# A gate taken third, state sums ahead of the convolution, and one product for both scan directions in the first layer

## The reference, cut to what matters

```python
xs, bm, cm = split(silu(conv5(x @ w_in[...]) + bias))  # 32 heads of 64, 8 groups of 4 heads, state 128
z = x @ w_in[...]                                      # the gates
xc = xs * dt                                           # dt differs between the two directions
cs = cumsum(dt * a)                                    # within chunks of 128 tokens
cb   = einsum('bclgn,bcsgn->bclsg', cc, bc)
lmat = exp(where(lower, cs[l] - cs[s], -inf))
y = einsum('bclsg,bclsgr,bcsgrp->bclgrp', cb, lmat, xc) \
  + einsum('bclgn,bcgrpn,bclgr->bclgrp', cc, h_in, exp(cs))
h = h * exp(cs_end) + einsum('...', bc, decay_to_end, xc)   # the state handed from chunk to chunk
ssd = rmsnorm((y_forward + y_backward + d * xs) * silu(z)) @ w_ssd_o
```

## Time and profile before

| | us |
|---|---|
| median of 3 runs | 2936.31 (2933.43 to 2937.91) |
| the profiled execution's own time | 2936.1 |
| its span, first to last instruction | 2934.3 |
| PE busy | 2833.2, 97% of the span |
| DVE busy | 871.6, 30% |
| ACT busy | 722.1, 25% |
| POOL busy | 325.7, 11% |

### The profile page before, as it was taken

How to read it: one execution, slowest core, us unless ns; L and a number is a source line. 1 busy time by engine, 2 the same in 40 slices (tenths; PEclk the granted TensorE clock), 3 DMA queues, 4 the chain that set the end, 5 groups by cost and what they waited for, 6 DMA issues and landing times.

```text
span 2934.3 us, 30410 instructions
## 1 busy us (share of the span) xinstructions
PE 2833.2 (97%) x12082; PEld 1794.3 (61%) x12082; DVE 871.6 (30%) x1656; ACT 722.1 (25%) x1696; POOL 325.7 (11%) x326
## 2 busy tenths in 40 slices
PE   7989998999999998999999999999999999999999
PEld 6778884555555565444444444444665677788888
DVE  1330005555455333200121000005667632211101
ACT  1330012555455333100010000003445422101100
POOL 3000001233233121000000000000122222000000
PEclk8999999999999999999999999999999999999999
DMA  9236775433332121222262442425444322357652
GB/s 235 81 100 186 196 199 135 115 101 98 87 101 67 51 58 44 58 79 79 72 179 74 129 131 75 129 75 132 115 103 108 91 67 73 96 153 222 173 151 86
DMA packets 530156, 330.37 MB, mean 113 GB/s; under 512 B 27504, under 2 KB 496864, under 8 KB 530016
## 3 DMA queue, kind: packets, MB, share of 16 engines
q1 hardware_dynamic: 519184, 296.36, 36.7%
q0 software_dynamic: 10528, 31.46, 4.4%
q10 hardware_dynamic: 304, 0.61, 0.1%
HBM read 327.05 MB, written 1.34 MB: 112 GB/s over the span
## 4 chain that ended last, share of the span: by engine, by line
PE 82%; ACT 8%; DVE 5%; issue 2%; PEld 1%; DMA 1%; DVEq 1%; POOL 0%; PEldq 0%; POOLq 0%; ACTq 0%; SPq 0%
PE ps L972 61%; PE ps L1345 4%; PE ps L1336 4%; PE ps L1327 3%; ACT TMP L797 2%; PE ps L1311 2%; DVE TMP L1870 2%; PE ps L1432 2%; PE ps L998 1%; PE ps L1455 1%; ACT TMP L803 1%; ACT BIG L809 1%; PE ps L982 1%; PEld ps L972 1%; DMA BIG<-bias_lines 1%
## 5 line engine op out<-in xcount | busy, mean ns | idle before, releaser
L972 PE MATMUL ps<-xnT,W 128*128 128x512 f32 (+2 forms) x4064 | 1327.3, 486 | 15.2 <-DVE TMP L1652 6.7
L972 PEld LDWEIGHTS ps<-xnT,W 128*128 128x128 f32 (+1 forms) x4064 | 771.7, 191 | 530.5 <-issue 448.1
L972 PE MATMUL ps<-BIG,W 128*128 128x256 f32 (+1 forms) x2528 | 772.4, 467 | 5.3 <-DVEq L401 2.7
L972 PEld LDWEIGHTS ps<-BIG,W 128*128 128x128 f32 x2528 | 480.4, 191 | 290.8 <-issue 245.9
L1870 DVE SCALAR_TENSOR_TENSOR TMP<-ps,prmT,TMP 128x510 f32<-128x510 f32 (+3 forms) x256 | 181.9, 714 | 106.1 <-ACT TMP L776 91.4
L612 ACT ACTIVATE xnT<-hT 128x512 f32<-128x512 f32 (+1 forms) x48 | 25.2, 525 | 563.4 <-DVE hT L1801 464.4
L1801 DVE SCALAR_TENSOR_TENSOR hT<-ps,modc,hT 128x256 f32<-128x256 f32 x48 | 21.8, 481 | 373.6 <-PE ps L972 373.6
L564 POOL TENSOR_TENSOR BIG<-BIG,TMP 128x512 f32<-128x512 f32 x80 | 106.6, 1348 | 191.5 <-ACT BIG L809 191.5
L2072 DVE TENSOR_TENSOR BIG<-TMP 128x512 f32<-128x512 f32 (+1 forms) x64 | 35.8, 559 | 301.8 <-ACT TMP L942 301.8
L1345 PE MATMUL ps<-W,xnT 128*128 128x128 f32 x1024 | 122.8, 276 | 0.0
L797 ACT ACTIVATE TMP<-BIG,TMP 128x128 f32<-128x128 f32 x384 | 117.4, 392 | 12.4 <-PE ps L1311 12.4
(11 more groups left out here) (274 smaller groups left out, 2144.3 us busy)
## 6 DMA issues: line engine op xcount, KB each, us to landing
W<-in_w_in SPq DMA_DIRECT2D x192, 512.0 KB, 4.0
W<-in_w_mlp SPq DMA_DIRECT2D x128, 512.0 KB, 4.1
W<-in_ada_w SPq DMA_DIRECT2D x96, 512.0 KB, 3.8
BIG<-cs_rows POOLq DMA_DIRECT2D x96, 256.0 KB, 4.8
W<-in_w_ssd_o SPq DMA_DIRECT2D x32, 512.0 KB, 3.7
W<-in_w_gate SPq DMA_DIRECT2D x22, 512.0 KB, 5.8
W<-in_w_up SPq DMA_DIRECT2D x22, 512.0 KB, 6.0
W<-in_w_down SPq DMA_DIRECT2D x16, 512.0 KB, 3.8
```

What stands on the lines that cost most here:

```text
L972: last = mm(dst, w[:, c, 0:m], rhs(k), start=k == 0, stop=k == total - 1)
```

## The change

Six edits. The first four are in layer 0 alone.

1. For groups 1 to 7, z0 is made third: x0, x1, z0, B, C, z1. Both gates then go to bank PS[0], where B's product goes too (`early_z`, `front_order`). The weights are ordered to match. z0 waits for the convolution of x0, B for the first gate, z1 for the convolution of B.
2. On ACT the first gate and the activation of x0 move ahead of `decays(g, 2)`.
3. Both directions go into one product: `xc` is copied, and `masked` takes layer 1's form (eight instructions of 128 columns and an addition instead of two of 512 columns).
4. On DVE `masked(g, 3)` moves ahead of `conv(g+1, 2)`.
5. In both layers `carried(g, 0)` and `decayed(g, 2)` move ahead of `conv(g+1, 0)` on DVE.
6. In both layers the last group's pieces of the attention head are spread differently on PE: between its `outputs` (two steps between the last two, and in layer 0 two more between the first two). Two buffers of the attention (`va0`, `qkt`) get a place of their own in SBUF in place of one that the gates use.

The two new functions:

```diff
+def early_z(l, g):
+
+    return l == 0 and g > 0
+
+
+def front_order(l, g):
+    return (0, 1, 4, 2, 3, 5) if early_z(l, g) else range(6)
```

ACT, in the loop over groups:

```diff
                         center(g + 1, 1)
+                        if l == 0:
+                            gated(g + 1, 0)
+                            activated(g + 1, 0)
...
-                        for t in range(4):
+                        for t in range(0 if l else 1, 4):
                             activated(g + 1, t)
-                        for t in range(2):
+                        for t in range(0 if l else 1, 2):
                             gated(g + 1, t)
```

PE, `front` and `outputs`:

```diff
                 def front(g, t):
-                    if t >= 2:
+                    b = 0 if early_z(l, g) and t == 5 else t % 2
+                    if early_z(l, g) and t == 4:
+                        R("conv", 4 * g + 1)
+                    elif early_z(l, g) and t == 5:
+                        R("conv", 4 * g + 3)
+                    elif early_z(l, g) and t == 2:
+                        R("gated", 2 * g + 1)
+                    elif t >= 2:
                         R("conv", 4 * g + t - 1)
                     elif g:
-                        R("gated", 2 * (g - 1) + t + 1)
+                        R("gated", 2 * (g - 1) + (2 if early_z(l, g - 1) else t + 1))
...
-                        for d in range(1 if l else 2):
-                            terms.append([(xc[:, d, ch, h * HD:(h + 1) * HD], mt[:, (2 * (n_ch * g + i) + d) % 4, h, :])
-                                          for h in (2 * pair, 2 * pair + 1)])
+                        terms.append([(xc[:, ch, h * HD:(h + 1) * HD], mt[:, (2 * (n_ch * g + i)) % 4, h, :])
+                                      for h in (2 * pair, 2 * pair + 1)])
```

PE, in the loop over groups:

```diff
                     if more:
                         front(g + 1, 1)
+                        if l == 0:
+                            front(g + 1, 4)
...
                     if l == 0:
                         outputs(g, 0)
+                        if not more:
+                            next(head0)
+                            next(head0)
                         outputs(g, 1)
                     states(g, 2)
                     if more:
                         front(g + 1, 2)
                         front(g + 1, 3)
                     else:
-                        for _ in range(4):
+                        for _ in range(2 if l == 0 else 4):
                             next(head0)
                     outputs(g, 0 if l else 2)
+                    if not more:
+                        next(head0)
+                        next(head0)
                     outputs(g, 1 if l else 3)
                     if more:
-                        front(g + 1, 4)
+                        if l:
+                            front(g + 1, 4)
                         front(g + 1, 5)
```

DVE, `masked` and the loop over groups:

```diff
-                        if l == 0:
-                            V.tensor_tensor(mt[:, c % 4, :, :], mt[:, c % 4, :, :],
-                                            cbm[:, d, order[i], :].unsqueeze(1).to_broadcast([P, 4, P]), ALU.mult)\
-                                .then_inc(ssd[l, "mready"], 1)
-                            continue
...
                     masked(g, 0)
+                    carried(g, 0)
+                    decayed(g, 2)
                     if more:
                         conv(g + 1, 0)
-                    carried(g, 0)
-                    decayed(g, 2)
                     dve.drain()
...
                     if l == 0:
                         masked(g, 2)
+                        masked(g, 3)
                     if more:
                         conv(g + 1, 2)
-                    if l == 0:
-                        masked(g, 3)
-                    if more:
                         conv(g + 1, 3)
```

More of the change, by code:

```diff
@@ L195, in weight_tiles @@
         for g in range(NG):
[L196 to L198 removed]
+            at = (SSD_X + g * 256, SSD_X + P + g * 256, SSD_B + g * P, SSD_C + g * P, SSD_Z + g * 256, SSD_Z + P + g * 256)
+            for t in front_order(l, g):
+                col(("ssd", l, g, FRONT[t]), wi, at[t])
         for h in range(8):
@@ L786, in gated @@
                         R("y1", 2 * (g - 2) + 2)
-                    A(zs[:, g % 2, t, 0:n_tok], PS[t][:, 0:n_tok], ACT.Silu).then_inc(ssd[l, "gated"], 1)
+                    b = 0 if early_z(l, g) else t
+                    A(zs[:, g % 2, t, 0:n_tok], PS[b][:, 0:n_tok], ACT.Silu).then_inc(ssd[l, "gated"], 1)
                 def decays(g, i):
@@ L1958, in _ @@
                         R("ychunk", n_ch * g)
[L1959 to L1968 removed]
+                    for b in range(n_ch // 2):
+                        last = V.tensor_copy(flat(xc[:, 2 * b:2 * b + 2, :]), PS[4 + b][:, :])
                     last.then_inc(ssd[l, "xc"], 1)
```

26 lines of the change are left out of this document (5 added, 21 removed).

## The result

The changed kernel takes 2903.24 us, median of 4 runs (2901.84 to 2906.13), and the kernel before took 2936.97 us, median of 4 (2933.43 to 2937.91), on the same chip. The ratio is 0.9889, with a 95% interval of 0.9871 to 0.9906: 1.1% faster. The forecast was 2901.7.

What follows compares the result with a forecast made beforehand. PE, busy 97% of the span, was taken as the bound. Terms 26.6 + 1.8 - 3.2 + 8.4 + 0.8 = 34.4 us came off 2936.1, giving 2901.7 us; the 8-in-10 range was 2894 to 2913.

Steps and rivals of the forecast that it cites:

- Less work on PE, 1.83 a group: Layer 0 output products: each group loses 32 records at 0.057 us each, saving 1.83 us.
- The waits, 2.60 + 0.2 - 0.2: Layer 0 groups: PE's waits before outputs go, 2.60 us, plus 0.2 of restarts, less 0.2 of new wait at z0.
- The sum of a group, 4.43: A layer 0 group saves 4.43 us from less work and fewer waits; six groups save 26.6.
- Does the rest of the group keep up?: Rest of a layer 0 group: 3.2 us of cover before z1 hides longer masks; up to 1 us stays as bound.
- The first rival: Layer 0 masks meet POOL's multiplications and become the bound, costing 1.5 to 2.5 us a group: 2911 to 2917 us; 12%.
- Group 0, 1.8: Layer 0's group 0 saves only the work on PE, 1.8 us, with no wait counted.
- The last group, -3.2: Layer 0's last group loses 3.2 us through a late third mask; the other bound was a gain of 0.6.
- Layer 1, 1.4 a group and 0.8 at the end: Layer 1: earlier third-state tokens save 1.4 us in each of six groups; covering the scores' wait for v saves 0.8.
- the signs that the forecast named: Profile after: layer 0 group 51.2 to 51.4 us, layer 1 38.4, z0 wait 0.1 to 0.3, last group's third-mask wait some 7.
- The waits only change place: In layer 0 z0 inherits the 2.6 us of waits, so only the work goes: 2915.5 us, or 2925 without layer 1; 8%.
- Slower: Masks meeting POOL eat the gains: slower by over 0.2% from 6.8 us a group, 2951 us at 8.2; 3%.
- the ring: Layer 0 dependency loop through masks, x0's convolution, z0, third decays, B's convolution, z1 and transposes; could lose 8.2 us a group.

Runs made afterwards that it cites:

- e9: The changed kernel with layer 0's two directions as two products again, with scaled copies and old masks; 53.15 us a layer 0 group, 2919.23 us in all.
- e2: The kernel before with only layer 0's two directions put into one product; 58.04 us a layer 0 group, 2961.98 us in all.
- e7: The changed kernel with the first gate put back last; 56.09 us a layer 0 group, 2932.93 us in all.
- e3: The kernel before with only the carried state and last scaling moved ahead of the first convolution on DVE, both layers; 54.46 us a layer 0 group, 2923.85 us.
- e1: The kernel before with only layer 0's first gate computed third and both gates through B's bank; 53.10 us a layer 0 group, 2921.0 us.
- e6: The changed kernel with the first convolution back ahead of the carried state and last scaling on DVE, both layers; 2914.75 us.
- e4: The changed kernel with the attention head's pieces in both layers' last groups spread as before the change; 2911.2 us, one run.
- e5: The changed kernel with POOL's rotation in layer 0's last group held until DVE's last mask there is made; 2903.8 us, one run.
- e11: The kernel before with one product in layer 0, plus thirty throwaway products on PE ahead of the second outputs of seven groups; 2968.82 us.
- e12: The changed kernel with third states, POOL's rotation and ACT's copy of k moved earlier in layer 0's last group; 2900.99 us.

## Why the prediction was right

- **Less work on PE, 1.83 a group.** 1.80 by e9 against after, 53.15 - 51.35 (1.74 by the five groups of 53.09). Right, but only where the masks are covered: alone it costs 2.34 (e2), and with states first but no early gate 1.63 (e7 against e3).
- **The waits, 2.60 + 0.2 - 0.2.** e1: 2.60 net. The forecast had the second mask ready at +22.2 from the transposes and PE asking at +24.9; it was 706.61 - 684.33 = +22.3 and 709.25 - 684.33 = +24.9. z0's new wait is 0.29 instead of 0.2. One reading was wrong without changing the sum: the 0.81 us were a wait for the first state and not for a mask (e3).
- **The sum of a group, 4.43.** Measured 4.35. That the terms of layer 0 add is true of this sum, with the early gate in it, and false otherwise: alone, the gate, the product and the states give -2.60, +2.34 and -1.24, which add up to -1.50; all three in one kernel give -4.35. My theory that each removes its own term fell for the product. The gate third is worth 2.60 us in the kernel before and 56.09 - 51.35 = 4.74 in the changed one.
- **Does the rest keep up?** It did. The third and fourth masks lose 2.0 us each to POOL, as the earlier trace rows had it for one pair; of 3.2 us of cover ahead of z1, 0.9 are left. The first rival was near.
- **Group 0, 1.8.** 2.4 measured. The forecast had no wait in it; the kernel before waits 0.40 us there for a mask, 19.69 us behind the transposes, and the changed one doesn't.
- **The last group, -3.2.** -1.95. The direction and the late third mask are right; the size of the wait and what sets the end are not. The forecast let POOL's rotation meet the third mask and had it end near +31.5. The rotation began at +28.1, just as the mask's instructions were through, and PE went on at +28.4, so the wait was 3.71 us and not some 7. The forecast then had PE's own work set the end, with the fourth mask ready near +35, in time. It was ready at +35.4 because the rotation stretched it, and PE waited 0.31 us for it: the fourth mask set the end, one `outputs` ahead of the scores at +36.9. The forecast also left out the clock, 0.50 from 918.15 to 920.91, where third outputs that take 1.4 us took 2.8. This cost nothing here, since PE had to wait for the fourth mask all the same.

```profile
918.15:920.91 2.76, 2.76 (x24) 2.43 (x24) 2.76 (x3) 0.00 (x0) 2.64 (x3) 0.50 0.00 0
```

- **Layer 1, 1.4 a group and 0.8 at the end.** 1.42, shown to be the states first by e3 and e6. 1.0 at the end, of which the spread is 0.7 to 0.8 (30.05 in e3 and 30.14 in e4 against 29.35). The rest goes with the clock: behind a wait of 2.65 us for the third state's tokens it was 0.52 over the next 3.4 us in the kernel before, and behind the same wait of 2.64 us it stayed at 1.00 in the changed one and in e3 and e4. The edits don't decide it: e5, whose layer 1 is that of the changed kernel, had the low clock there and 29.63 at the end.
- **The total.** The parts give -34.3 against -34.4, but with +2.8 ahead of the scans that belongs to no edit, so the terms themselves gave some 2 us more than forecast (last group, group 0) and about 1 comes from untouched parts. That closeness is partly luck. Of the signs that the forecast named, both groups' lengths and z0's wait came as said; the last group's wait was there at half the size.
- **Rivals.** "The waits only change place": no, z0 waits 0.29. "Slower": the ring that I named had 0.9 us left. What would have made the change slower was another thing, not among the rivals: the one product without cover, as e2 shows.

## What to carry to other kernels

Price a cover by what returns when it is gone, and add the lower clock behind a long wait of TensorE: the 3.5 us that the gate covers cost 5.0 on average, and only themselves in the one group where the clock stayed up. An edit that saves work on the busy engine by giving another more can lose by itself and win beside one that moves the deadline, so try such edits in pairs before one is dropped. At the end of a loop, where the covering work is gone, the same edit needs its own order of the pieces (7.7 us here).

## What the runs showed of the hardware

- A wait of some microseconds can cost more than itself. Waits of 2.98, 3.71, 3.89, 3.96 and 4.70 us were each followed by a granted clock of about half, and records took up to twice as long for some 3 to 7 us. Of the six waits of 3.47 and 3.48 us in e7, two were followed by it at once, three some 1.5 us later, and one not at all. With the wait filled, the clock stayed at 1.00 (e11). The Trainium skill (TensorE: Matmul & The Clock Gate, HAM oscillation — how this bites in real kernels) describes the same for waits on DMA. These rows agree but for that one, here for waits on VectorE inside a stream that is otherwise full.
- Shorter waits went both ways. The clock stayed at 1.00 behind 1.79 and 2.08 us in the kernel before and 2.64 in the changed one. It fell behind 2.65 in the kernel before, at the same place of the program as the 2.64; behind 2.08 in e3 (first scores 2.08 us instead of 1.13); and, 1.4 us later, behind 1.99 in e12. So the length of the wait alone doesn't decide. What does is not settled here.
- Eight DVE instructions of 128x128 with both inputs in SBUF take 2.19 us alone, 4.2 beside two POOL multiplications, and 6.3 beside POOL's rotation; shown by taking the rotation away (e5).
